# All key, query and gate projections in token form, turned by DMA, with GpSimd splitting the planes

## What is computed

```python
h = rms_norm(x, norm_gain)                      # (256, 2048)
qa, ka, va, ga, qb, kb, vb, gb, qi, ki, wi = split(h @ w_in)      # eight parts of 1024, index parts 1024, 64, 16
out_a = chunked attention(qa, ka, va) + learned relative bias      # 8 heads of 128, chunks of 64
score = sum over 16 index heads of wi * relu(qi . ki)              # index head width 64
out_b = attention(qb, kb, vb) over the 64 best keys of each query, less slope * distance   # 8 heads
y = concat(out_a * silu(ga), out_b * silu(gb))
out = rms_norm(x + y @ w_out, final_gain)
```

## Time and profile before

| what | value |
|---|---|
| median of 3 runs | 521.59 us (521.5 to 522.29) |
| profiled execution | 520.91 us, of which the recorded span is 518.8 |
| TensorE matmul busy | 509.6 us, 98% |
| TensorE weight load busy | 442.2 us, 85% |
| VectorE, ScalarE, GpSimd busy | 364.7, 306.1, 31.1 us |
| granted TensorE clock | 0.998 of full over the span |
| share of the 16 DMA engines in SP's queue | 63.3% |

### The profile page before, as it was taken

How to read it: one execution, slowest core, us unless ns; L and a number is a source line. 1 busy time by engine, 2 the same in 40 slices (tenths; PEclk the granted TensorE clock), 3 DMA queues, 4 the chain that set the end, 5 groups by cost and what they waited for, 6 DMA issues and landing times.

```text
span 518.8 us, 7543 instructions
## 1 busy us (share of the span) xinstructions
PE 509.6 (98%) x2736; PEld 442.2 (85%) x2736; DVE 364.7 (70%) x544; ACT 306.1 (59%) x415; POOL 31.1 (6%) x47
## 2 busy tenths in 40 slices
PE   8999999999999999999999999999999999999994
PEld 6989999888888888888888888888888878888883
DVE  5798776775856787867776776687878778646554
ACT  6876555446564554445675849495868676544342
POOL 1000054140400000000000000000000000000000
PEclk9999999999999999999999999999999999999999
DMA  8984787758795776553956575665647875576614
GB/s 276 356 261 134 241 262 257 245 176 244 230 271 163 251 215 222 179 190 99 284 145 228 158 228 167 190 192 163 198 159 231 288 230 171 195 207 200 198 42 162
DMA packets 83933, 107.79 MB, mean 208 GB/s; under 512 B 26400, under 2 KB 68288, under 8 KB 83648
## 3 DMA queue, kind: packets, MB, share of 16 engines
q1 hardware_dynamic: 82320, 101.92, 63.3%
q0 software_dynamic: 1296, 5.01, 3.0%
q10 hardware_dynamic: 288, 0.46, 0.2%
HBM read 99.24 MB, written 2.11 MB: 195 GB/s over the span
## 4 chain that ended last, share of the span: by engine, by line
PE 97%; DMA 1%; DVE 0%; issue 0%; ACT 0%; DVEq 0%; POOLq 0%
PE acc L506 28%; PE acc L475 14%; PE acc L477 14%; PE acc L476 14%; PE acc L510 14%; PE acc L526 4%; PE acc L534 3%; PE aux L536 2%; PE aux L658 1%; PE aux L667 1%; DMA gain<-norm_gain 1%; PE aux L655 0%; PE aux L656 0%; PE aux L673 0%; PE aux L654 0%; PE aux L672 0%
## 5 line engine op out<-in xcount | busy, mean ns | idle before, releaser
L1068 DVE TENSOR_TENSOR lo_slots<-raw_slots,hi_slots 128x1024 fp32r<-128x1024 f32 x166 | 204.7, 1240 | 105.1 <-ACT hi_slots L735 103.8
L735 ACT ACTIVATE hi_slots<-raw_slots 128x1024 fp32r<-128x1024 f32 x166 | 174.3, 1056 | 140.7 <-PE acc L477 91.3
L506 PE MATMUL acc<-acts,hi_slots 128*128 128x512 f32 (+1 forms) x640 | 195.5, 387 | 0.0
L510 PEld LDWEIGHTS acc<-acts,lo_slots 128*128 128x128 f32 x640 | 119.3, 188 | 22.7
L475 PE MATMUL acc<-hi_slots,acts 128*128 128x512 f32 x320 | 124.9, 390 | 0.7 <-issue 0.7
L476 PE MATMUL acc<-lo_slots,acts 128*128 128x512 f32 x320 | 124.6, 389 | 0.0
L477 PE MATMUL acc<-hi_slots,acts 128*128 128x512 f32 x320 | 124.5, 389 | 0.0
L510 PE MATMUL acc<-acts,lo_slots 128*128 128x256 f32 (+1 forms) x640 | 123.8, 275 | 0.0
L506 PEld LDWEIGHTS acc<-acts,hi_slots 128*128 128x128 f32 x640 | 97.4, 189 | 0.1
L475 PEld LDWEIGHTS acc<-hi_slots,acts 128*128 128x128 f32 x320 | 60.1, 188 | 13.0 <-issue 0.9
L477 PEld LDWEIGHTS acc<-hi_slots,acts 128*128 128x128 f32 x320 | 60.1, 188 | 12.6
(11 more groups left out here) (179 smaller groups left out, 478.0 us busy)
## 6 DMA issues: line engine op xcount, KB each, us to landing
raw_slots<-w_blocks SPq DMA_DIRECT2D x140, 512.0 KB, 4.4
raw_slots<-wo_blocks SPq DMA_DIRECT2D x32, 512.0 KB, 4.2
raw_slots<-w_blocks SPq DMA_DIRECT2D x8, 256.0 KB, 5.3
qk<-x POOLq DMA_DIRECT2D x1, 2048.0 KB, 10.7
qk<-xT SPq DMA_DIRECT2D x7, 256.0 KB, 5.3
o<-ext_dram POOLq DMA_DIRECT2D x1, 1024.0 KB, 10.0
fgain<-final_gain POOLq DMA_DIRECT2D x1, 1024.0 KB, 8.0
out<-o SPq DMA_DIRECT2D x2, 512.0 KB, 3.0
```

Source lines behind the costliest of these rows:

```text
L506: nc.tensor.matmul(whole, w_hi4[:, u % RING, q, f * HD:f * HD + HD], acts[:, k, :, tokens], start=(k == 0), stop=False)
L510: last = nc.tensor.matmul(acc[:, bank:bank + n], w_lo4[:, u % RING, q, f * HD:f * HD + HD], a_hi[:, k, tokens], start=False, stop=(k == KT ...
L735: nc.scalar.activation(hi_slots[:, s, 0:UK * CB], w_raw[:, s, :], ACT.Copy).then_inc(hi_done, 1)
L1068: nc.vector.tensor_tensor(lo_slots[:, s, 0:UK * CB], w_raw[:, s, :], hi_slots[:, s, 0:UK * CB].bitcast(f32), ALU.subtract).then_inc(lo_don ...
```

## The change

All blocks from 10 to 17 go from feature form to token form, and each of their results is turned by DMA as those of blocks 4 to 7 were. In detail:

- TensorE runs `unit` in place of `feature_unit` in the eight pair blocks; the scores come after unit 1 and the value product after unit 0 as before. A block waits for the drain of the block before the last.
- ScalarE no longer copies `low` halves or splits the probabilities' planes. It drains each block (`projection_out`) behind the third unit of the next block's splits, joins it (`join_projection`) after the sixth, and then copies `output`; after that come the next pair's exponentials. A gate block's drain waits until the gates before it have been used (`y_done`).
- VectorE no longer adds halves nor multiplies by `rk`, and `rk`'s root and reciprocal are gone; the norm of a token is a per-partition scale of the drain.
- GpSimd splits the planes of the probabilities and of the eight late projections, in the order in which they come. The residual's load moves behind one of these splits.
- SP turns the probabilities' planes behind the load of unit 2 in place of ahead of it, and turns each projection behind the load of unit 6.
- For the gates `z` is the home of the turned words, `v1` (its first half) and `t_gate` hold the planes. The tanh takes both halves in one instruction. The last gates are turned while the output projection runs; `y_hi(q)` waits for q+1 units of block 17 and not for six or eight.

The core of the diff:

```diff
@@ SP
+            def token_block(g, row, pair=None, n=None):
                 for u in range(UNITS):
                     sp.wait_ge(lo_done, g * UNITS + (u - RING + 1))
                     load(u, w_blocks[ds(row, 1), u, :, :].rearrange("o p c -> (o p) c"))
+                    if u == 2 and pair is not None:
+                        turn_planes(pair)
+                    if u == 6 and n is not None:
+                        turn_projection(n)
@@ GpSimd
+            def split_projection(n):
+                pool.wait_ge(proj_out, n + 1)
+                nc.gpsimd.tensor_copy(proj_planes(n)[0], halves(z)).then_inc(proj_split, 1)
+                pool.wait_ge(proj_split, n + 1)
+            def split_planes(pair):
+                pool.wait_ge(normed, pair + 1)
+                nc.gpsimd.tensor_copy(planes, halves(probs)).then_inc(planes_made, 1)
+                pool.wait_ge(planes_made, pair + 1)
+            split_planes(0)
+            for n in range(N_LATE, N_END):
+                split_projection(n)
+                if n == N_END - 2:
+                    pool.wait_ge(scored, HEADS)
+                    pool.dma_start(x_flat.rearrange("p (m d) -> p m d", m=TM), x).then_inc(res_landed, 16)
+                if n < N_END - 1:
+                    split_planes(n - N_LATE + 1)
@@ TensorE
-                pe.wait_ge(feat_out, 2 * g - 17)
-                feature_unit(g, 0)
-                if pair > 0:
-                    value_pair(pair - 1)
-                feature_unit(g, 1)
+                for u in range(UNITS):
+                    unit(g, u)
+                    if u == 0 and pair > 0:
+                        value_pair(pair - 1)
+                    if u == 1:
+                        pe.wait_ge(proj_joined, (4, 4, 4, 4, 7, 7, 8, 8)[pair])
+                        score_pair(pair, 2 * pair + 1 if pair < 4 else pair)
@@ ScalarE
+            def pair_attention(g, pair, staged):
+                exps(pair, pair < 4)
                 split_hi(g, 6)
                 split_hi(g, 7)
+                if pair > 4:
+                    tanh_gates(pair - 5)
                 split_hi(g, 8)
                 split_hi(g, 9)
+                stage_q(*staged)
+                pT_out(pair)
                 split_hi(g, 10)
+                if pair > 4:
+                    act.wait_ge(y_done, 2 * (pair - 4))
+                projection_out(g)
                 split_hi(g, 11)
                 split_hi(g, 12)
                 split_hi(g, 13)
+                join_projection(pair + N_LATE)
+                act.wait_ge(proj_joined, pair + N_LATE + 1)
+                output(pair)
@@ y_hi
-                act.wait_ge(mm_done, (G_OUT - 1) * UNITS + (6 if q < 4 else 8))
+                act.wait_ge(mm_done, (G_OUT - 1) * UNITS + q + 1)
```

More of the change, by code:

```diff
@@ L257, in hybrid_block @@
         AUX1_INDEX, AUX1_PAIRS = 1, 5
+        N_LATE, N_GATE, N_END = 4, 8, 12
         AUX3_PAIRS = 1
@@ L392, in _ @@
             for g in range(G_TOKENS, G_VA):
-                token_block(g, g - G_QI if g < G_VB else ROW_VB + 1, g - G_TOKENS - 1 if g > G_TOKENS else None)
+                token_block(g, g - G_QI if g < G_VB else ROW_VB + 1, n=g - G_TOKENS - 1 if g > G_TOKENS else None)
             token_block(G_VA, ROW_VA)
-            feature_block(G_QKA, G_QKA)
-            for g in range(G_QKA + 1, G_OUT):
-                feature_block(g, g, g - (G_QKA + 1))
+            token_block(G_QKA, G_QKA)
+            for pair in range(HEADS - 1):
+                g = pair + G_QKA + 1
+                token_block(g, g, pair, pair + N_LATE)
             def out_unit(g, u):
@@ L852, in projection_out @@
                                                 acc[:, bank:bank + CB].rearrange("p (f t) -> p f t", f=4), ACT.Copy,
-                                                scale=rstd[:, m:m + 1] if keys else 1.0)
+                                                scale=1.0 if queries else rstd[:, m:m + 1])
                 last.then_inc(proj_out, 1)
@@ L929, in exps @@
                 last.then_inc(exp_done, 1)
-            def planes_out(pair):
-                act.wait_ge(normed, pair + 1)
-                nc.scalar.activation(planes, halves(probs), ACT.Copy).then_inc(planes_made, 1)
             def pT_out(pair):
@@ L1017, in _ @@
             y_hi(5)
-            tanh_gate(3, 1)
-            y_hi(6)
             split_hi(G_OUT, 4)
             split_hi(G_OUT, 5)
-            output(7)
+            output(HEADS - 1)
+            join_projection(N_END - 1)
+            tanh_gates(3)
+            split_hi(G_OUT, 6)
+            y_hi(6)
+            split_hi(G_OUT, 7)
             y_hi(7)
-            split_hi(G_OUT, 6)
-            split_hi(G_OUT, 7)
             nc.scalar.preload_act_table(ACT.Sqrt)
@@ L1470, in gated, with probabilities @@
                 nc.vector.scalar_tensor_tensor(y, t_gate[:, half, :], 1.0, y, ALU.add, ALU.mult).then_inc(y_done, 1)
-            def gate_block(g, i, next_pair):
-                bias_a(i)
-                maxima(i + 4, False)
-                normalise(i + 4)
+            def probabilities(pair):
+                if pair < 4:
+                    bias_b(pair)
+                else:
+                    bias_a(pair - 4)
+                maxima(pair, pair < 4)
+                normalise(pair)
+            for pair, staged in enumerate(((2, 3), (4, 5), (6, 7), (0, 4), (1, 5), (2, 6), (3, 7))):
+                g = pair + G_QKA
+                probabilities(pair)
@@ L1496, in y_lo @@
+                pT_rest(pair)
+                for c in range(10, 14):
+                    split_lo(g, c)
             def y_lo(q):
@@ L1500, in y_lo @@
                                         a_hi[:, UK * q:UK * q + UK, :].bitcast(f32), ALU.subtract).then_inc(ylo_done, 1)
-            gate_block(G_OUT - 1, 3, False)
-            for q in range(4):
-                y_lo(q)
+            g = G_OUT - 1
+            probabilities(HEADS - 1)
+            split_lo(g, 6)
+            split_lo(g, 7)
+            gated(2, 0)
+            gated(2, 1)
+            split_lo(g, 8)
+            y_lo(0)
+            y_lo(1)
+            split_lo(g, 9)
+            y_lo(2)
+            y_lo(3)
+            split_lo(g, 10)
             pT_rest(HEADS - 1)
-            gate_out(G_OUT - 1, 3, 1)
             split_lo(G_OUT, 3)
```

228 lines of the change are left out of this document (73 added, 155 removed).

## The result

The changed kernel takes **534.0 us** (median of 6 runs, 533.35 to 537.07), the kernel before 521.6 in the same measurement; the ratio is 1.025, 95% interval 1.023 to 1.027. Slower by 2.5%, where 518.7 was forecast and the range ended at 531.5. The profiled run took 533.35 us, with a span of 531.6 (before: 518.8).

What follows compares the result with a forecast made beforehand. TensorE, busy 98% of the span and holding 97% of the chain, was taken as the bound. 520.91 - 4.3 - 0.8 + 0.3 + 0.6 + 1.3 gave 518.0, plus 0.7 for the median 518.7 us; range 516.2 to 531.5.

Steps and rivals of the forecast that it cites:

- Part 1: Matmuls of the eight late blocks in token form: 4.3 us off the path, a pair's block from 24.62 to 24.08.
- the ring: Order on ScalarE tying one pair's exponentials to the next pair's: 24.0 us, against a block of 24.08.
- Part 2: Start of the output projection: TensorE's idle stretch until the first `y_lo` goes, 0.8 us off.
- The copy's own price: GpSimd's split copies at 0.87 ns an element: 1.9 us for a projection, 1.45 us for the probabilities' planes.
- (b): Rival: GpSimd's copy costs as a two-input instruction, ring 28.3 us, 545 us; chance 0.11 together with worse mixtures of (a).
- the 1.3 ns form of (a): GpSimd's copies at 1.3 ns an element make the ring 25.5 us: 527.7 us; within (a)'s chance of 0.31.
- (a): Rival: the ring is longer than the block and stalls each pair, 527.7 or 526.8 us; chance 0.31.
- VectorE's own split comes first and GpSimd waits for it, 1.13: In each pair, GpSimd's planes copy waits 1.13 us, for one VectorE split only.
- the paragraph on the lock: Shared use by VectorE and GpSimd: a copy or split that starts first delays the other by up to its own length.
- The turn: SP's DMA turns in the ring: 4.3 us for a projection, 3.7 for the planes.
- The end: Last gate block, ahead of `y_lo(0)`: 0 to 2.5 us of stall, 1.3 taken.

Runs made afterwards that it cites:

- e4: Changed kernel without GpSimd's copy and SP's turn of the eight late projections, so it computes something else: 518.6 us, ratio 0.993.
- e7: Changed kernel with ScalarE's projection join and output copy moved behind units 6 and 7 of the next pair, GpSimd keeping both copies: 518.5 us, ratio 0.993.
- e6: Changed kernel with ScalarE's join and output copy moved behind units 6 and 7 of the next pair, and planes split on VectorE: 517.2 us, ratio 0.992.
- e2: Changed kernel in which VectorE waits before its first weight split of a pair (unit 6) until GpSimd has split the planes: 532.1 us, ratio 1.020.
- e1: Changed kernel in which VectorE waits after its first weight split of a pair (unit 6) until GpSimd has split the planes: 529.9 us, ratio 1.014.
- e5: Changed kernel with no late copy on GpSimd: ScalarE splits the probabilities' planes, VectorE the late projections: 518.6 us, ratio 0.994.
- e9: Changed kernel with a two-column memset on VectorE between the splits of units 6 and 7 in pairs 0 to 6: 521.0 us, ratio 0.999.
- e11: e6 with every late projection split twice on GpSimd: 539.2 us, ratio 1.035.
- e3: Changed kernel with the probabilities' planes split on ScalarE behind unit 6, GpSimd keeping the projections' copies: 522.8 us, ratio 1.002.

## Why the prediction was wrong

**Part 1 was right, a little large.** A pair went from 24.62 to 24.15 us in e4 to e7, where the ring does not hold TensorE up (24.08 forecast).

**Part 2 was right.** In e4, e6 and e7 TensorE has no wait at the start of the output projection, and from the next-to-last value product to the last it is 26.87 us, where it was 28.26. In the changed kernel it is 28.62, with a wait of 1.0 us for `y_lo`: there the gain was lost, as the prediction had allowed for. Together with part 1 the span falls by 3.5 us in e6 (518.8 to 515.3), a stall of 0.3 us included, so the two parts gave 3.8 of the 5.1 us forecast. Some 0.4 us of what is missing was lost ahead of block 10, where the change leaves the matmuls as they were: pair 0's scores start at 232.31 where they started at 232.04, though two of the cheaper units lie before them.

**The copy's own price was right.** 1.90 and, undisturbed in e2, 1.47 us (1.9 and 1.45 forecast): with the 0.13 us of one element taken off, 0.86 and 0.87 ns an element. It was a choice between rows of other operations, so some luck is in it. The first worry of the prediction, the price of an operation no row had shown, was no problem at all. Rivals (b), the two-input price, and the 1.3 ns form of (a) are out.

**The step that failed** is the line "VectorE's own split comes first and GpSimd waits for it, 1.13", and the paragraph on the lock that repeats it. I took it that the one who asks gets the port when the instruction in progress ends. It was 2.1 to 5.3 us instead, 3.2 in the mean: GpSimd waits for the end of VectorE's run of two-input instructions. With it the exponentials came every 25.3 to 28.7 us in place of 24.0 (e1, with the assumed order in force, has 24.0 to 24.1 where the turn is on time). It may also feed itself, which no constant term can express: a late ring lets more weights be ready, so that VectorE's run is longer, so that the copy is later. The run was two or three splits where nothing was late and six instructions in pair 1; but in pair 2, which was later still, it was two, so this is a reading and not shown.

The Trainium skill (SBUF — State Buffer, section Who interferes with whom) says that the port pair which VectorE and GpSimd share is an exclusive lock held for the whole instruction, and that the order of issue decides who blocks. The first half agrees with the rows here. The second does not: GpSimd's copy of pair 1 starts in the trace at 268.69, before VectorE's second split, and ended 1.32 us behind VectorE's sixth instruction.

**The turn was a second, smaller mis-size.** I took 4.3 us and gave 5.7 to rival (a). Late turns took 4.3 to 5.8 us to the join in the changed kernel, and up to 6.7 (e5) and 9.0 (e9) in the variants; in e11 one landed after 19.1. e3, whose planes copy is not on GpSimd, still takes 4 us more than e5, and most of its stalls stand in pairs 5 to 7, where the turns are 5.8 and 6.5.

**The end was about right.** I allowed 1.3 us; in the changed kernel TensorE's waits from 430 us on are 1.4 (1.0 and 0.4, both for `y_lo`). The same place is where e1 lost 5.6 us at once, which no term had.

**The rival was the right one, its price too low.** (a) named the mechanism, ring longer than block, and gave 526.8 or 527.7. Of the 15.5 us between the spans of the changed kernel and e4 (531.6 and 516.1), TensorE's waits from pair 0 on are 11.8 less e4's 1.5, so 10.3. The lower clock behind the longest wait is 2.5 more: the 22 matmuls from the value product on take 6.23 us there and 3.68 in e6. The granted clock had no term in any of my sums, though a ring that makes TensorE wait 4 us at a time calls for one. The other 2.7 stand at the same waits: by the distance between value products the changed kernel loses 14.6 us to e4 from the first to the last (186.5 against 171.9), and each wait costs 0.2 to 0.7 us more than the idle time listed for it.

Two statements of cause are shown, not argued: that the run of splits keeps GpSimd out (e9, one memset and nothing else), and that in the changed kernel its lateness is handed from pair to pair by the ring (e7, one reordering on ScalarE and nothing else, though it also shortens the run). It can cost outside the ring too: 1.5 us in pair 0 of the changed kernel and of e7, and 5.6 us before the last gates in e1. Not settled is what makes a turn land in 4.3 or in 5.8 us. Two turns of e5 with weight loads issued at the same distance, 1.15 us ahead of them, took 4.8 and 5.9 us to the join; I have no run that sets this alone.

## What to carry to other kernels

When an engine shares something exclusively with another, price the wait by the other's whole run of such instructions, not by one of them, and ask whether being late could make that run longer; where the wait is on the path, put one harmless instruction in the run, or an order that breaks it. Before adding a step to a chain, write down whether the chain closes on itself from one iteration to the next: an engine's program order (here a join ahead of the next exponentials) closes it as surely as data does, and moving one call opened it and was worth 15 us. A sum whose terms are read one by one holds for an open chain; for a closed one near the length of its block, every term needs its worst row, and TensorE's waits need the clock that follows them.

## What the runs showed of the hardware that I had not expected

- GpSimd, waiting with a copy, does not get in between VectorE's two-input instructions that follow each other directly: a copy that reads 1.47 us undisturbed read 2.33, 3.46, 4.6 and 6.68 us behind one, two, three and six of them, and one of 1.9 us up to 8.57. The first ended 1.32 to 1.33 us behind the last of them each time. A pause of VectorE's of 0.2 us (299.56 to 299.76 in the changed kernel) let it in. A memset of 0.06 us between two of them lets it in.
- A transposing DMA with a 2 MB load issued 0.28 us behind it took 19.1 us to land instead of 4.3, and held its queue for 11.87 us. With the load issued after it had landed: 4.2 and 10.2 us.
- Splitting 1536 halves of 16 bits took 0.96 us on VectorE (e6), 1.47 on GpSimd (e2) and 1.49 on ScalarE (e3).
- Behind a wait of 3.9 us TensorE's matmuls of 512 columns came every 0.43 us for 3 us, against 0.23: the granted clock was 0.50 there, 1.2 GHz instead of 2.4.
